# Statistics matmul of the norm behind the fourth instead of the second weight unit, in another PSUM bank

## The chip, the core and the metric

One core of a Trainium2 chip runs the whole kernel as one program. The metric is the device time in microseconds (us); three runs of the kernel before gave 2397.48, 2397.86 and 2401.97 us, median 2397.86 us.

## The reference, cut to what matters

512 tokens of width 1024 go through two blocks in a row. The first has an attention mixer, a SwiGLU feed-forward block, a second attention mixer and a second SwiGLU; the second has a gated linear recurrence and a retention layer. All is float32.

```
def rmsnorm(x, g):
    y = x * rsqrt(mean(x * x, -1) + RMS_EPS) * g
def swiglu(h, w_gu, w_down):
    gu = h @ w_gu;  g, u = gu[..., :D_FF], gu[..., D_FF:]      # D_FF = 2816
    return (silu(g) * u) @ w_down
# feed-forward, twice:      h = h + swiglu(rmsnorm(h, ffn_norm[i]), ...)
# retention, once:          h = rms_norm(x, norm_pre[1]);  u = h @ w_in   (q, k, v, gate of 4 heads)
```

Each norm needs, for every token, the sum of squares over the 1024 channels. The kernel multiplies by the gain before the matmul and by the token's reciprocal root after it, on the matmul's result. So the matmuls that use the normed x can begin before the sum of squares is known; only their evacuation from PSUM needs it.

## The kernel before, in words

**Layout.** The residual R is kept transposed: 8 tiles (k = 0 to 7) of 128 channels x 512 tokens. Each version of it is scaled by a gain and split in two float32r parts: XH (the high part, ScalarE, L1055) and XL (the rest, VectorE, L1560). A product takes three matmuls: high x high, low x high, high x low.

**Weights.** They come as "units" of 128 x 1024 float32 (512 KB). SyncE loads them in order into a ring of RING = 5 slots WR (L496); unit u may load once unit u-5 has been used (semaphore unit_used). ScalarE makes the high half WH (L1046), VectorE the low half WL (L1554). Both do so at places written out by hand: `split(end)` handles all units below `end` that have not been handled, and waits for each of them in order.

**TensorE.** `unit` (L505) runs one unit: 2 tiles k, 4 banks o, 3 matmuls each, so 24 matmuls of 128 x 128 x 512, all from L523. `group` runs several units that accumulate into the same 4 of the 8 PSUM banks. `x_ready` makes a group wait, tile by tile, for XH and XL. `between` is a table of calls made between units of a group. In both SwiGLU blocks (`swiglu(layer, ...)`) 11 groups of 4 units (units f+0 to f+43) are run, alternating between banks 0-3 and 4-7; layer 0 starts with banks 0-3, layer 1 with 4-7. The retention layer runs for each of 4 heads three groups of 4 units, the first into its `own` banks (0-3 for head 0), the second into the `other` banks.

**Sum of squares.** GpSimd squares the eight tiles of R one after the other and adds them up in SQS (`squares`, L1405 to L1411). `statistics` on TensorE waits until that is done (sq_sum) and multiplies SQS by a matrix of ones (L540), which puts the sum over the partitions into a PSUM bank; for the retention layer 8 narrow matmuls (L543) also put it, token by token on the partitions, into the bank behind it. VectorE reads both (`variance`, L1571), which raises rb_var; ScalarE takes the root (`root`, L1060), VectorE the reciprocal (`rstd`, L1575). Engines work strictly in program order, so `statistics` stops TensorE, if the squares are not there yet, and everything written behind it waits.

**Order around the change.** In group 0 of a SwiGLU `statistics` stands behind the second unit and writes into the first bank of the next group. Before group 1 TensorE waits for rb_var, since that group overwrites the bank. VectorE handles units up to f+5, reads the variance, takes the reciprocal, and only then units f+6 and f+7; ScalarE does likewise. In the retention layer it is the same with units R+0 to R+3, banks 6 and 7, and rb_var 8 awaited ahead of head 0's second group.

Of the kernel before, what the change touches and what calls it, by code (L numbers as in the profile page):

```python
# [13 lines left out]
T = 512  # L14
# [42 lines left out]
def program(nc, ws, x, vec, cst, sel, turn_a, turn_r, decay, post1, out):  # L57
    with ExitStack() as ctx:
# [13 lines left out]
        R = sb("R", [P, DT, T])  # L72
# [429 lines left out]

        @block.tensor
        def _(pe):
            def unit(u, kpair, hi, lo, bank, first, last, stationary, ready=None):  # L505

                s = u % RING
                pe.wait_ge(lo_ready, u + 1)
                for kk in range(2):
                    k = 2 * kpair + kk  # L510
                    if ready is not None:
                        ready(k)
                    for o in range(4):
                        if stationary:
                            cols = slice(kk * T + o * P, kk * T + (o + 1) * P)
                            pairs = [(WH[:, s, cols], hi[:, k, :]), (WH[:, s, cols], lo[:, k, :]),
                                     (WL[:, s, cols], hi[:, k, :])]
                        else:
                            cols = slice(kk * T, (kk + 1) * T)
                            xh, xl = stationary_x(hi, k, o), stationary_x(lo, k, o)  # L520
                            pairs = [(xh, WH[:, s, cols]), (xh, WL[:, s, cols]), (xl, WH[:, s, cols])]
                        for i, (l, r) in enumerate(pairs):
                            mm = pe.matmul(PS[:, bank + o, :], l, r, start=first and kk == 0 and i == 0,  # L523
                                           stop=last and kk == 1 and i == 2)
                mm.then_inc(unit_used, 1)
# [1 line left out]
            def stationary_x(t, k, o):  # L527
                return t[:, k, o * P:(o + 1) * P]

            def group(u, kpairs, hi, lo, bank, stationary=True, ready=None, between=None):  # L530

                for j in range(kpairs):
                    unit(u + j, j, hi, lo, bank, j == 0, j == kpairs - 1, stationary, ready)
                    if between is not None and j in between:
                        between[j]()

# [174 lines left out]
            for q in range(4):  # L711
# [6 lines left out]
                for kk in range(2):  # L718
# [12 lines left out]
                    for e in SPOT.get((6, 8 + 2 * q + kk), ()):  # L731
                        attend(e)

            def swiglu(layer, v, s):
                f, dn = U[f"F{layer}"], U[f"D{layer}"]
                first = 4 * layer
                for j in range(11):
                    n = 11 * layer + j
                    if j == 1:
                        pe.wait_ge(rb_var, s + 1)  # L740
                    if j >= 2:
                        pe.wait_ge(u_ready, n - 1)
                    group(f + 4 * j, 4, XH, XL, first if j % 2 == 0 else 4 - first, ready=x_ready(v),
                          between=None if j else {1: lambda: statistics(s, 4 - first)})
                pe.wait_ge(u_ready, 11 * layer + 10)

                def hidden(k):
                    pe.wait_ge(hh_ready, 11 * layer + k // 2 + 1)
                    pe.wait_ge(hl_ready, 11 * layer + k // 2 + 1)
                for d in range(2):  # L750
                    if d:
                        pe.wait_ge(u_ready, 11 * layer + 11)
                    group(dn + 11 * d, 11, HH, HL, first if d else 4 - first, ready=hidden)
# [232 lines left out]
            for h in range(RH):  # L986
                u = U["R"] + 12 * h
                own, other = own_banks(h), 4 - own_banks(h)

                group(u, 4, XH, XL, own, ready=x_ready(7),  # L990
                      between={1: lambda: outputs_turned(h - 1)} if h else {1: lambda: statistics(7, 6, (0,))})
                pe.wait_ge(rb_var, 8)
                if h:
                    pe.wait_ge(yl_ready, 4 * h)
                    pe.wait_ge(yh_ready, 4 * h)
                group(u + 4, 4, XH, XL, other, stationary=False)
                pe.wait_ge(rr_step, 4 * h + 4)
                group(u + 8, 4, XH, XL, own, stationary=False)
                pe.wait_ge(rr_ready, 4 * h + 4)
                pe.wait_ge(rsg_ready, 4 * h + 4)  # L1000
                pe.wait_ge(rg_ready, 4 * h + 4)
                for kb in range(TB):
                    for c in range(2):
                        mm = pe.matmul(PS[:, other + kb, 0:T - kb * P], R_QK[:, 2 + c, kb * P:(kb + 1) * P],
                                       R_QK[:, c, kb * P:T], start=c == 0, stop=c == 1)
                    mm.then_inc(rs_done, 1)
                pe.wait_ge(rv_ready, 4 * h + 4)
                for qb in range(TB):
                    pe.wait_ge(rpt_ready, 4 * h + qb + 1)
                    for kb in range(qb + 1):  # L1010
                        mm = pe.matmul(PS[:, own + qb, :],  # L1011
                                       R_PT[:, PT0[kb] + (qb - kb) * P:PT0[kb] + (qb - kb + 1) * P],
                                       R_V[:, kb, :], start=kb == 0, stop=kb == qb)
                    mm.then_inc(ro_done, 1)
# [23 lines left out]
        def _(act):  # L1038
            halved = [0]

            def split(end):

                for u in range(halved[0], min(end, UNITS)):
                    s = u % RING
                    act.wait_ge(landed[s], LANDED[u])
                    nc.scalar.activation(WH[:, s, :], WR[:, s, :], ACT.Copy).then_inc(hi_ready, 1)  # L1046
                halved[0] = max(halved[0], end)
# [100 lines left out]

            def swiglu(layer, s):
                f, dn = U[f"F{layer}"], U[f"D{layer}"]  # L1150
                split(f + 6)
                root(s)
                for j in range(11):
                    n = 11 * layer + j
                    split(f + 4 * j + 8)
                    act.wait_ge(g_ready, n + 1)
                    if j:
                        act.wait_ge(gs_ready, n)
                    nc.scalar.activation(F_S[:, :, :], F_G[:, :, :], ACT.Sigmoid).then_inc(sg_ready, 1)
                    act.wait_ge(ht_ready, n + 1)  # L1160
                    nc.scalar.activation(HH[:, 2 * j:2 * j + 2, :], F_U[:, :, :], ACT.Copy).then_inc(hh_ready, 1)
                split(dn + 15)
# [172 lines left out]
            for h in range(RH):  # L1335
# [4 lines left out]
                else:  # L1340
                    act.wait_ge(r_done, 56)
                act.dma_start(R_D[:, :], decay[h]).then_inc(decay_in, 16)
                split(u + 6)
                if h:
                    outputs_high(h - 1)
                else:
# [197 lines left out]
        def _(dve):  # L1544
# [22 lines left out]

            def variance(s, bank, width=T):
                dve.wait_ge(stat_done, s + 1)
                v = PS[:, bank:bank + 2, :].rearrange("p b t -> p (b t)")  # L1570
                ts(RB[:, 0:width], v[:, 0:width], 1.0 / D, RMS_EPS, ALU.mult, ALU.add).then_inc(rb_var, 1)  # L1571

            def rstd(s, width=T):
# [219 lines left out]
            def swiglu(layer, s):  # L1793
                f, dn = U[f"F{layer}"], U[f"D{layer}"]
                first = 4 * layer
                split(f + 6)
                variance(s, 4 - first)
                rstd(s)
                rb2 = RB[:, 0:T].unsqueeze(1).to_broadcast([P, 2, T])

                def low(j):
                    dve.wait_ge(hh_ready, 11 * layer + j + 1)
                    tt(HL[:, 2 * j:2 * j + 2, :], F_U[:, :, :], HH[:, 2 * j:2 * j + 2, :].bitcast(F32),
                       ALU.subtract).then_inc(hl_ready, 1)
                for j in range(11):
                    n = 11 * layer + j
                    bank = first if j % 2 == 0 else 4 - first
                    u = f + 4 * j
                    if j:
                        split(u + 6)  # L1810
                        low(j - 1)
                    split(u + 8)
                    dve.wait_ge(unit_used, u + 4)
                    tt(F_G[:, :, :], PS[:, bank:bank + 2, :], rb2, ALU.mult).then_inc(g_ready, 1)
                    if j:
                        dve.wait_ge(hl_ready, n)
                    tt(F_U[:, :, :], PS[:, bank + 2:bank + 4, :], rb2, ALU.mult).then_inc(u_ready, 1)
                    dve.wait_ge(sg_ready, n + 1)
                    tt(F_G[:, :, :], F_G[:, :, :], F_S[:, :, :], ALU.mult).then_inc(gs_ready, 1)  # L1819
                low(10)  # L1820
                return dn
# [248 lines left out]
            x_low(7, "pre1", 7)  # L2070


            split(U["R"] + 6)
            variance(7, 6, T + 4)
            rstd(7, T + 4)
            dve.wait_ge(rotr_in, 32)
# [195 lines left out]
```

## Time and profile before

| | |
|---|---|
| median of 3 runs | 2397.86 us |
| profiled execution, its own time | 2400.79 us |
| its span in the trace | 2399.0 us |
| mean granted TensorE clock | 0.971 of 2.4 GHz |
| PE busy (matmul) | 2247.3 us, 94% |
| DVE (VectorE) busy | 1222.0 us, 51% |
| ACT (ScalarE) busy | 798.3 us, 33% |
| POOL (GpSimd) busy | 532.7 us, 22% |
| DMA | 198.27 MB, mean 83 GB/s |

PE's busy time is of pipelined matmuls with modelled ends: a float32r matmul of 512 columns reads 0.39 us, but the next starts 0.227 us after it. So distances between starts say more than durations. Behind the span lie 1.8 us (2400.79 - 2399.0) of the execution that the trace does not cover.

### The profile page before, as it was taken

What the parts mean: (1) busy time and instruction counts of PE and PEld (TensorE: products, weight loads), DVE (VectorE), ACT (ScalarE), POOL (GpSimd) and SP (SyncE); (2) the same over time, 40 slices, a digit from 0 to 9 for tenths busy, and PEclk for the clock granted to TensorE, in tenths of its full rate; (3) what the DMA queues carried; (4) which work ended last, traced back from release to release, by engine and by line L of the source; (5) the groups of instructions that cost most, each with busy time, mean ns of one, the idle gap of its engine ahead of it and who ended that gap; (6) DMA issues with size and microseconds to landing.
All of it is one profiled execution on the core that took longest, in us unless ns stands there. A gap on an engine that the chain in (4) does not pass through costs nothing.

```text
span 2399.0 us, 26711 instructions
## 1 busy us (share of the span) xinstructions
PE 2247.3 (94%) x10598; PEld 1801.3 (75%) x10598; DVE 1222.0 (51%) x1987; ACT 798.3 (33%) x1334; POOL 532.7 (22%) x355
## 2 busy tenths in 40 slices
PE   7999999998899999999998999998994969999997
PEld 6788876886688888876666888887773748777876
DVE  5655556565544433554455444326858664444342
ACT  3334323442322222233432222213446423333321
POOL 2533334231410101222233011034125030000000
PEclk9999999998999999999999999999997989999999
DMA  4222221221233333332222333332331212222322
GB/s 139 88 62 80 80 80 54 71 80 45 71 97 97 97 97 98 96 97 89 71 61 72 97 97 97 98 97 79 94 91 44 79 57 88 75 75 78 93 74 76
DMA packets 84155, 198.27 MB, mean 83 GB/s; under 512 B 7216, under 2 KB 44208, under 8 KB 84032
## 3 DMA queue, kind: packets, MB, share of 16 engines
q1 hardware_dynamic: 81408, 189.62, 26.0%
q10 hardware_dynamic: 2624, 6.93, 0.9%
q8 instruction: 86, 1.41, 0.2%
q14 instruction: 37, 0.30, 0.0%
HBM read 194.40 MB, written 2.13 MB: 82 GB/s over the span
## 4 chain that ended last, share of the span: by engine, by line
PE 81%; DVE 9%; issue 4%; ACT 3%; POOL 3%; DMA 0%; DVEq 0%; SPq 0%; POOLq 0%; ACTq 0%
PE PS L523 49%; PE PS L567 5%; PE PS L569 5%; PE PS L568 5%; PE PS L592 2%; PE PS L593 2%; PE PS L594 2%; PE PS L1011 1%; PE PS L640 1%; PE PS L650 1%; PE PS L664 1%; DVE WL L1554 1%; POOL SQS L1411 1%; POOL SQT L1409 1%; PE PS L879 1%
## 5 line engine op out<-in xcount | busy, mean ns | idle before, releaser
L1554 DVE TENSOR_TENSOR WL<-WR,WH 128x1024 fp32r<-128x1024 f32 x353 | 475.2, 1354 | 786.3 <-ACT WH L1046 785.6
L1046 ACT ACTIVATE WH<-WR 128x1024 fp32r<-128x1024 f32 x353 | 370.0, 1056 | 732.2 <-DMA WR<-in_ws 723.1
L523 PE MATMUL PS<-XH,WH 128*128 128x512 f32 x1024 | 406.7, 397 | 18.9 <-ACT XH L1055 10.5
L523 PE MATMUL PS<-XL,WH 128*128 128x512 f32 x1024 | 402.3, 393 | 0.0
L523 PE MATMUL PS<-XH,WL 128*128 128x512 f32 x1024 | 402.0, 393 | 0.0
L523 PEld LDWEIGHTS PS<-XH,WH 128*128 128x128 f32 x1024 | 195.0, 190 | 65.1 <-issue 20.4
L567 PE MATMUL PS<-XH,WH 128*128 128x512 f32 x544 | 224.1, 412 | 5.0 <-DVE WL L1554 3.6
L523 PEld LDWEIGHTS PS<-XL,WH 128*128 128x128 f32 x1024 | 194.9, 190 | 41.6 <-issue 1.7
L523 PEld LDWEIGHTS PS<-XH,WL 128*128 128x128 f32 x1024 | 194.5, 190 | 41.2
L569 PE MATMUL PS<-XH,WL 128*128 128x512 f32 x544 | 214.6, 395 | 0.0
L568 PE MATMUL PS<-XL,WH 128*128 128x512 f32 x544 | 214.1, 393 | 0.0
L1466 POOL TENSOR_TENSOR F_U<-F_G,F_U 128x1024 f32<-128x1024 f32 x22 | 52.7, 2393 | 424.0 <-DVE F_G L1819 424.0
L1444 POOL TENSOR_TENSOR A_SH<-A_SH,A_SIN 128x512 f32<-128x512 f32 x48 | 82.2, 1713 | 268.9 <-DVE A_SH L1739 268.9
L523 PE MATMUL PS<-HH,WH 128*128 128x512 f32 x352 | 136.9, 389 | 0.0
L523 PE MATMUL PS<-HL,WH 128*128 128x512 f32 x352 | 136.9, 389 | 0.0
L523 PE MATMUL PS<-HH,WL 128*128 128x512 f32 x352 | 136.9, 389 | 0.0
L567 PEld LDWEIGHTS PS<-XH,WH 128*128 128x128 f32 x544 | 104.0, 191 | 27.4 <-issue 4.6
L1076 ACT ACTIVATE A_P<-A_P,A_ST 128x128 f32<-128x128 f32 (+1 forms) x192 | 79.7, 416 | 132.0 <-DVE A_ST L1682 132.0
L569 PEld LDWEIGHTS PS<-XH,WL 128*128 128x128 f32 x544 | 103.3, 190 | 23.2
L568 PEld LDWEIGHTS PS<-XL,WH 128*128 128x128 f32 x544 | 103.8, 191 | 18.9
L523 PE MATMUL PS<-WH,XH 128*128 128x512 f32 x256 | 99.6, 389 | 0.0
L523 PE MATMUL PS<-WL,XH 128*128 128x512 f32 x256 | 99.6, 389 | 0.0
(332 smaller groups left out, 3771.5 us busy)
## 6 DMA issues: line engine op xcount, KB each, us to landing
WR<-in_ws SPq DMA_DIRECT2D x281, 512.0 KB, 3.6
WR<-in_ws SPq DMA_DIRECT2D x144, 256.0 KB, 3.2
B_CB<-gates ACTq DMA_DIRECT2D x8, 512.0 KB, 3.9
XTOK<-in_x SPq DMA_DIRECT2D x2, 1024.0 KB, 8.3
out<-OUT SPq DMA_DIRECT2D x4, 512.0 KB, 2.6
R_D<-in_decay ACTq DMA_DIRECT2D x4, 256.0 KB, 2.6
GAIN<-in_post ACTq DMA_DIRECT2D x1, 512.0 KB, 5.4
CST<-in_cst SPq DMA_DIRECT2D x1, 320.0 KB, 3.4
```

The lines of the kernel that those rows point to most:

```text
L523: mm = pe.matmul(PS[:, bank + o, :], l, r, start=first and kk == 0 and i == 0, stop=last and kk == 1 and i == 2)
L567: pe.matmul(PS[:, bank + o, :], WH[:, s, cols], hi[:, k, :], start=first, stop=False)
L568: pe.matmul(PS[:, bank + o, :], WH[:, s, cols], lo[:, k, :], start=False, stop=False)
L569: return pe.matmul(PS[:, bank + o, :], WL[:, s, cols], hi[:, k, :], start=False, stop=last)
L592: pe.matmul(PS[:, o, :], xh, wh, start=first and kk == 0, stop=False)
L593: pe.matmul(PS[:, o, :], xh, wl, start=False, stop=False)
L594: mm = pe.matmul(PS[:, o, :], xl, wh, start=False, stop=last and kk == 1)
L1046: nc.scalar.activation(WH[:, s, :], WR[:, s, :], ACT.Copy).then_inc(hi_ready, 1)
L1076: x = nc.scalar.activation(A_P[:, n % 2, h, w], A_P[:, n % 2, h, w], ACT.Exp, bias=stat(m, 0, 2 * pair + h, qb), accum_out=stat(m, 1, 2 * ...
L1444: nc.gpsimd.tensor_tensor(A_SH[:, r % 2, :], A_SH[:, r % 2, :], A_SIN[:, :], ALU.mult).then_inc(rot_m, 1)
L1466: nc.gpsimd.tensor_tensor(F_U[:, :, :], F_G[:, :, :], F_U[:, :, :], ALU.mult).then_inc(ht_ready, 1)
L1554: tt(WL[:, s, :], WR[:, s, :], WH[:, s, :].bitcast(F32), ALU.subtract).then_inc(lo_ready, 1)
```

## The change

In both SwiGLU blocks and in the retention layer `statistics` is called behind the fourth unit of the first group instead of behind the second (`between` index 3 instead of 1). In the SwiGLU blocks it writes into the last bank of the next group (7 in layer 0, 3 in layer 1) instead of the first (4 and 0). The wait for rb_var is no longer ahead of the next group: `unit` calls `free(o)` before the first matmul into each bank, and the wait is made only at the bank that holds the sums (o = 3 in the SwiGLU blocks; o = 2, which is bank 6, in the retention layer). ScalarE and VectorE handle the weight units up to f+7 (R+7) instead of f+5 (R+5) before root and variance. `variance` reads one bank instead of naming two where only 512 columns are used.

```diff
-            def unit(u, kpair, hi, lo, bank, first, last, stationary, ready=None):
+            def unit(u, kpair, hi, lo, bank, first, last, stationary, ready=None, free=None):
...
                     for o in range(4):
+                        if free is not None and first and kk == 0:
+                            free(o)
...
+            def variance_read(o, count):
+
+                def wait(bank):
+                    if bank == o:
+                        pe.wait_ge(rb_var, count)
+                return wait
+
             def swiglu(layer, v, s):
...
-                    if j == 1:
-                        pe.wait_ge(rb_var, s + 1)
                     if j >= 2:
                         pe.wait_ge(u_ready, n - 1)
                     group(f + 4 * j, 4, XH, XL, first if j % 2 == 0 else 4 - first, ready=x_ready(v),
-                          between=None if j else {1: lambda: statistics(s, 4 - first)})
+                          between=None if j else {3: lambda: statistics(s, 7 - first)},
+                          free=variance_read(3, s + 1) if j == 1 else None)
...
                 group(u, 4, XH, XL, own, ready=x_ready(7),
-                      between={1: lambda: outputs_turned(h - 1)} if h else {1: lambda: statistics(7, 6, (0,))})
-                pe.wait_ge(rb_var, 8)
+                      between={1: lambda: outputs_turned(h - 1)} if h else {3: lambda: statistics(7, 6, (0,))})
...
-                group(u + 4, 4, XH, XL, other, stationary=False)
+                group(u + 4, 4, XH, XL, other, stationary=False, free=None if h else variance_read(2, 8))
...
             def swiglu(layer, s):                       # ScalarE
-                split(f + 6)
+                split(f + 8)
                 root(s)
...
-                split(u + 6)
+                split(u + 6 if h else u + 8)
...
             def variance(s, bank, width=T):
-                v = PS[:, bank:bank + 2, :].rearrange("p b t -> p (b t)")
+                v = PS[:, bank:bank + 1 + (width > T), :].rearrange("p b t -> p (b t)")
...
             def swiglu(layer, s):                       # VectorE
-                split(f + 6)
-                variance(s, 4 - first)
+                split(f + 8)
+                variance(s, 7 - first)
...
-            split(U["R"] + 6)
+            split(U["R"] + 8)
             variance(7, 6, T + 4)
```

## Rows read from the trace of the kernel before

**Rows 1.** The page: shares of the chain that ended last, by engine
```profile
PE 81%; DVE 9%; issue 4%; ACT 3%; POOL 3%; DMA 0%; DVEq 0%; SPq 0%; POOLq 0%; ACTq 0%
```
**Rows 2.** Waits of PE: who for whom, us in total, times, longest us
```profile
PE PS L540 <- POOL SQS L1411: 28.6, 3, 10.9
```
**Rows 3.** Timeline, PE, layer 0: start us, duration us, operation [idle before, releaser]
```profile
625.73 0.39 PE L523 MATMUL PS<-XH,WL 128*128 128x512 f32 x1
634.81 2.07 PE L540 MATMUL PS<-SQS,CST 128*128 128x512 f32 x2 [8.69 <-POOL SQS L1411]
...
637.86 0.39 PE L523 MATMUL PS<-XH,WH 128*128 128x512 f32 x1
...
642.39 0.39 PE L523 MATMUL PS<-XH,WL 128*128 128x512 f32 x1
```
**Rows 4.** Timeline, PE and DVE, layer 1: the same place
```profile
1267.28 0.39 PE L523 MATMUL PS<-XH,WL 128*128 128x512 f32 x1
1276.75 2.07 PE L540 MATMUL PS<-SQS,CST 128*128 128x512 f32 x2 [9.08 <-POOL SQS L1411]
...
1283.34 0.39 PE L523 MATMUL PS<-XH,WH 128*128 128x512 f32 x1
...
1270.20 4.26 DVE L1554 TENSOR_TENSOR WL<-WR,WH 128x1024 fp32r<-128x1024 f32 x2
```
**Rows 5.** Timeline, PE, retention layer: tile k = 3, the statistics, the second group
```profile
1960.40 0.47 PE L523 MATMUL PS<-XH,WH 128*128 128x512 f32 x1 [0.81 <-ACT XH L1055]
...
1974.24 2.08 PE L540 MATMUL PS<-SQS,CST 128*128 128x512 f32 x2 [10.87 <-POOL SQS L1411]
...
1990.95 0.39 PE L523 MATMUL PS<-WH,XH 128*128 128x512 f32 x1
```
**Rows 6.** The chain in order of time, the piece behind layer 0's statistics: start, us
```profile
636.88 348.62 PE PS L523 x1536
```
**Rows 7.** Timeline, PE: the second attention's statistics, which meet no wait
```profile
1001.66 1.02 PE L540 MATMUL PS<-SQS,CST 128*128 128x512 f32 x2
1002.52 0.95 PE L543 MATMUL PS<-CST,SQS 128*128 128x1 f32 x8
...
1003.64 0.39 PE L568 MATMUL PS<-XL,WH 128*128 128x512 f32 x1
```
**Rows 8.** Timeline, DVE and ACT, layer 0: lowered units, variance, unit f+7
```profile
626.86 4.26 DVE L1554 TENSOR_TENSOR WL<-WR,WH 128x1024 fp32r<-128x1024 f32 x2
636.92 0.69 DVE L1571 TENSOR_SCALAR RB<-PS 128x512 f32<-128x512 f32 x1 [5.80 <-PE PS L540]
...
646.19 1.06 ACT L1046 ACTIVATE WH<-WR 128x1024 fp32r<-128x1024 f32 x1 [6.97 <-DMA WR<-in_ws]
```
**Rows 9.** Tile SQS: the adds on POOL, ns shortest/median/longest, first and last start us
```profile
L1411 POOL TENSOR_TENSOR SQS<-SQS,SQT x28: 1260/1620/2163, 613.7 to 1972.6; 128x512 f32<-128x512 f32 x28
```
**Rows 10.** Timeline, DVE, retention layer: XL of k = 3, 5, 6, 7, then two units
```profile
1959.51 0.74 DVE L1560 SCALAR_TENSOR_TENSOR XL<-R,VC,XH 128x512 fp32r<-128x512 f32 x1
...
1967.10 0.74 DVE L1560 SCALAR_TENSOR_TENSOR XL<-R,VC,XH 128x512 fp32r<-128x512 f32 x1
...
1970.87 0.74 DVE L1560 SCALAR_TENSOR_TENSOR XL<-R,VC,XH 128x512 fp32r<-128x512 f32 x1
1971.74 1.32 DVE L1560 SCALAR_TENSOR_TENSOR XL<-R,VC,XH 128x512 fp32r<-128x512 f32 x1
1973.43 2.97 DVE L1554 TENSOR_TENSOR WL<-WR,WH 128x1024 fp32r<-128x1024 f32 x2 [0.37 <-ACT WH L1046]
```
**Rows 11.** DMA issues from 1960 to 1985 us: count, KB each, median us to landing
```profile
WR<-in_ws SPq DMA_DIRECT2D x1, 512.0 KB, 3.5
...
R_D<-in_decay ACTq DMA_DIRECT2D x1, 256.0 KB, 3.7
```
**Rows 12.** Windows, retention layer: length, busy PE, PEld, DVE, ACT, POOL; clock, DMA, GB/s
```profile
1956.00:1963.00 7.00, 5.66 (x25) 4.35 (x24) 6.93 (x6) 1.26 (x2) 6.06 (x4) 1.00 0.26 77
1977.50:1982.50 5.00, 5.00 (x13) 3.95 (x14) 3.96 (x2) 1.58 (x2) 0.00 (x0) 0.50 0.00 0
```

More of the change, by code:

```diff
@@ L528, in stationary_x, with group @@
                 return t[:, k, o * P:(o + 1) * P]
-            def group(u, kpairs, hi, lo, bank, stationary=True, ready=None, between=None):
+            def group(u, kpairs, hi, lo, bank, stationary=True, ready=None, between=None, free=None):
                 for j in range(kpairs):
-                    unit(u + j, j, hi, lo, bank, j == 0, j == kpairs - 1, stationary, ready)
+                    unit(u + j, j, hi, lo, bank, j == 0, j == kpairs - 1, stationary, ready, free)
                     if between is not None and j in between:
```

## Prediction, made before the changed kernel was run

> **What bounds the kernel now.** I first read the chain of work that ended last: 81% of the span is TensorE (PE) work [rows 1], so a microsecond counts where PE stands still, or runs at its low clock. Next came the waits of PE. The longest is that of `statistics` (L540) for the sum of squares that GpSimd (POOL) adds up (L1411): 28.6 us in three places [rows 2]. The timelines give each place. In layer 0 the last matmul of the second unit starts at 625.73 and the next thing PE does is L540 at 634.81, the moment POOL is done [rows 3]; in layer 1 it is 1267.28 and 1276.75 [rows 4]; in the retention layer PE waits from the end of tile k = 3 until 1974.24 [rows 5]. What stands behind L540 in PE's order are the third and fourth unit of the group, which need nothing of the sum. So the reader is to see three holes with ready work queued behind them. Each hole also has a tail: PE restarts at its low clock. From 1977.50 to 1982.50 the granted clock is 0.50, that is 1.2 GHz, and 13 matmuls take 5.00 us [rows 12].
>
> **The pace of PE.** At the high clock (2.4 GHz) 20 starts take 642.39 - 637.86 = 4.53 us [rows 3], so a slot is 0.2265 us, a tile (12 matmuls) 2.72 us and a unit (24) 5.44 us.
>
> **Layer 0.** Without the wait the third unit starts at 625.73 + 0.23 = 625.96, and its fourth matmul at 625.96 + 3 x 0.2265 = 626.64. Before, that matmul starts at 637.86 [rows 3]: 11.22 us lost, which is 8.85 of standing and 2.37 of cold statistics and restart. Now the statistics run behind the fourth unit on a warm PE. There L540 takes 1002.52 - 1001.66 = 0.86 us up to the next start [rows 7]. Gain 11.22 - 0.86 = 10.36 us.
>
> Are the inputs there? The XL tiles are all done by 626.86, when VectorE (DVE) starts the two units behind them [rows 8]; the last tile, k = 7, is needed at 625.96 + 3 x 2.72 = 634.12. The units f+2 and f+3 were lowered before f+4 and f+5. The fourth unit ends at 625.96 + 2 x 5.44 = 636.84; POOL is done at 634.81. Margin 2.0 us, so `statistics` no longer waits.
>
> **Layer 1.** The thirteenth matmul behind the hole starts at 1283.34; without it, it would start at 1267.51 + 12 x 0.2265 = 1270.23 [rows 4]. Lost: 13.11 us. Gain 13.11 - 0.86 = 12.25 us. Tile 7 is ready at 1270.20 [rows 4] and needed at 1275.7; the fourth unit ends at 1278.39, POOL at 1276.75: margin 1.6 us.
>
> **Retention layer.** Here X itself comes slowly: DVE makes an XL tile every 3.8 us, more than the 2.72 us that PE needs for it. PE starts a tile 0.15 us behind XL's end (1959.51 + 0.74 = 1960.25, PE at 1960.40) [rows 5, 10]. So tile 5 starts at 1967.84 + 0.15 = 1967.99 and ends at 1970.71; tile 6 starts at 1971.61 + 0.15 = 1971.76 and ends at 1974.48; tile 7 (XL done at 1973.06) follows at once and ends at 1977.20. POOL has been done since 1974.24: here the hole goes because X ends last, 3 us later than POOL. Statistics with the 8 narrow matmuls cost, warm, 1003.64 - 1001.66 - 0.23 = 1.75 us [rows 7]. The second group starts at 1978.95, before at 1990.95 [rows 5]. Gain 12.0 us.
>
> **The wait that is moved.** rb_var is now awaited inside the next group, ahead of the bank with the sums, and DVE has to get there first. Behind that wait PE has the whole rest of the group. DVE's order is now: units f+6 and f+7, then the variance. f+7 may load only when unit f+2 has been used (ring of 5). In layer 0 that unit ends at 631.57 (start of its last matmul + 0.39). Before, the same step took 646.19 - (642.39 + 0.39) = 3.41 us from release to ScalarE's (ACT) start [rows 3, 8], and a weight load lands in 3.5 us [rows 11]. So ACT starts f+7 at 634.98, and is done at 636.04; DVE lowers it in 1.2 to 2.1 us (a contended one is 4.26 / 2 = 2.13 [rows 8]; POOL is finished, so I take 1.2) to 637.3. PE ends the statistics at 637.86 at the latest, the variance takes 0.69 us [rows 8]: rb_var at 638.6. PE is at bank 3 (9 matmuls on) at 637.70 + 2.04 = 639.74. Margin 1.1 us, the same in layer 1: cost nothing. The load, cast and lowering of f+6 come forward too, off the path. In the retention layer unit R+2 ends at 1970.9, and ACT issues three 256 KB tables just then. Alone, R+7 lands in 3.5 us (1974.4); behind one of them it would take 3.5 + 3.7 = 7.2 us (1978.1) [rows 11]. DVE has R+4 and R+5 done at 1976.40 [rows 10], R+6 and R+7 at 1978.8 if landed early, 1980.5 if late. rb_var is then up at 1979.7 or at 1981.2, and PE is at bank 6 (6 matmuls on) at 1978.95 + 1.36 = 1980.31. Cost 0 to 0.9 us; I take 0: R+7 was released 0.1 us ahead of the tables, so it is nearer to the 3.5 us of a load alone.
>
> The waits at the banks themselves are checked at three places between matmuls; x_ready puts two ahead of every tile of a first group, and the 0.2265 us pace has them in it. I take nothing for them, at most 0.1 us. Less reading of PSUM in `variance` changes nothing, since its output stays 512 wide.
>
> **Beside POOL.** What comes forward on DVE is the lowering of f+6 at 631.1, beside POOL's last instructions. An add on POOL takes 1.26 us alone and 2.16 at its longest [rows 9]; if the last two instructions both grow by 0.9, POOL ends at 636.6 in layer 0, still ahead of 636.84. In layer 1 only the last add can grow: 1277.7 against 1278.39. Cost nothing.
>
> The Trainium skill speaks against that: SBUF — State Buffer, section "Who interferes with whom", says that DVE with two SBUF inputs and GpSimd take a shared port pair as an exclusive lock, the second fully blocked. By that rule two of POOL's instructions would each wait out one lowering of 1.2 us, POOL would end 0.4 us behind PE in layer 0, and the gain would be smaller by that. The row of adds, 1.26 to 2.16, agrees with waiting of that size, so the rule moves the end by tenths only.
>
> **What follows behind.** PE's work behind layer 0's statistics is one unbroken piece of 348.62 us [rows 6]; all that feeds it is released by PE itself, so it moves forward whole. Next to be late would be u_ready, group 0's evacuation, which the third group awaits. Before, DVE began it behind unit f+7, at 646.19 + 1.06 + 1.2 = 648.5 [rows 8]. Even if it stayed there, that is 11 us ahead of the third group's new start at 637.70 + 4 x 5.44 = 659.5.
>
> **The sum.** 10.36 + 12.25 + 12.0 = 34.6 us. The profiled execution took 2400.79 us and would take 2366.2. The median of the runs is 2.9 us below it; the three gains are taken off it alike: 2397.86 - 34.6 = 2363.3 us.
>
> **The rivals.**
>
> A: PE loses its clock in the retention layer. With tiles fed every 3.8 us PE pauses about 1.1 us ahead of each. Before, it did so at k = 2 and 3 too, and the clock from 1956 to 1963 was 1.00 with PE busy 5.66 of 7 us [rows 12]; that speaks against it. For it: the pauses now go on over tiles 4 to 6. Price: at 13 matmuls in 5.00 us (a wave of 0.43 us at half clock) a tile takes 5.1 us, more than the 3.8 of X, so tiles 4 to 7 end at 1964.2 + 4 x 5.1 = 1984.6 instead of 1977.2, 7.4 us later: 2370.7 us.
> The Trainium skill has such a rule: TensorE: Matmul & The Clock Gate, section "A second HAM failure mode: psum-queue depth-cycling", tells that frequent micro-idles between groups of matmuls make the clock swing. The row at 1.00 does not bear it out here.
>
> B: the weights come late for the variance, so that the old wait is replaced by one inside the next group. Price 0.9 us in the retention layer, by the bounds above, and perhaps 1 more in each feed-forward block: up to 2366 us.
>
> C: the time is given back: PE arrives early somewhere where another engine sets the pace. For it: ACT and DVE do the same work in less time. Against: they are busy 33% and 51%, and the unbroken piece [rows 6]. Price: all, 2397.9 us.
>
> D, slower than before: the variance on DVE now stands behind unit f+7, whose load is released only by the third unit of the same group. If it lands late, PE stands at bank 3 just as long. From 3.5 + 1.1 = 4.6 us on each us costs one; at 4.6 + 11.5 = 16.1 us the gain is gone in each of the three places; at 20 us it would be 3.9 us slower in each, 2409.6 us. Against it: loads land in 3.5 us, the slowest of these rows in 3.7 [rows 11].
>
> E: the change does not do what it says, if POOL ended later than the fourth unit. The margins are 2.0, 1.6 and 3.0 us.
>
> **Chances.** Forecast 0.79, A 0.07, B 0.09 (a shift of 1 to 3 us), C 0.03, D 0.02; E only shrinks the gain and lies in the forecast's range. Range: the cold tails vary with the phase of the clock, 2.37 us in layer 0 against 13.11 - 9.24 = 3.87 in layer 1. Were all tails like the long one, the gain would be 1.5 us larger; like the short one, some 3 smaller. The runs of before differ by 4.5 us. So 2360.0 to 2369.0 us. What a measurement of this kernel can tell from no change is about 0.2%, 4.8 us; faster by more 0.95, within 0.03, slower 0.02.
>
> **What would show it.** Right: no wait of L540 for L1411 longer than 0.5 us; the matmuls of third and fourth unit at 0.227 us from the second; L540 at 1.02 us instead of 2.07; the retention layer's statistics at 1977.2 less the 22.6 us gained earlier, that is 1954.6; clock 1.00 in the three stretches. Wrong: PE waiting for RB at bank 3 or 6 (B, D); a clock of 0.50 ahead of the retention statistics (A); new waits of L523 for WL or for u_ready (C).

## The result

The changed kernel takes 2364.72 us (median of 4 runs, 2361.93 to 2366.95), the kernel before 2398.64 us (4 runs, 2397.48 to 2401.97): ratio 0.9856, 95% interval 0.9839 to 0.9873. It is 33.9 us faster; the prediction said 34.6 (2363.3 us, range 2360.0 to 2369.0). The profiled execution took 2365.22 us, its span is 2363.4 us. The line numbers are those of the changed kernel: L540 is now L542, L523 L525, L1411 L1418, L1554 L1561, L1571 L1578.

The page of the changed kernel: busy time by engine, then the chain by engine. PE is as busy in us as before, within 9 us of 2247.3; POOL has gone from 3% of the chain [rows 1] to 0%, "issue" from 4% to 2%.

```profile
PE 2238.7 (95%) x10598; PEld 1797.5 (76%) x10598; DVE 1225.6 (52%) x1987; ACT 798.2 (34%) x1334; POOL 536.0 (23%) x355
...
PE 85%; DVE 9%; ACT 3%; issue 2%; DMA 0%; POOL 0%; DVEq 0%; SPq 0%; ACTq 0%
```

The waits of PE, longest first (who for whom, total us, times, longest). The wait of `statistics` for POOL, 28.6 us before [rows 2], is in no line any more, and none for RB at L1578 has taken its place. What is first now stood second before, in the recurrence; the wait for XH (three waits, 10.5 us) has grown to five of 12.0 us together, by the pauses between tiles in the retention layer.

```profile
PE PS L961 <- ACT L_R L1295: 14.8, 1, 14.8
PE PS L525 <- ACT L_IB L1295: 14.8, 1, 14.8
PE PS L525 <- ACT XH L1062: 12.0, 5, 9.2
```

The timeline of PE and DVE in layer 0, to be held against [rows 3, 8]. The statistics (L542) follow the fourth unit without a gap and take 1.02 us, not 2.07; the second group's second matmul is at 639.70, one slot of 0.23 us behind where its first belongs (638.61 + 0.86 = 639.47). DVE reads the variance from 639.66 to 640.35, while PE is at bank 3 only at 641.55.

```profile
638.37 0.40 PE L525 MATMUL PS<-XH,WL 128*128 128x512 f32 x1
638.61 1.02 PE L542 MATMUL PS<-SQS,CST 128*128 128x512 f32 x2
639.06 0.80 PE L525 MATMUL PS<-XH,WH 128*128 128x512 f32 x1
639.70 0.40 PE L525 MATMUL PS<-XL,WH 128*128 128x512 f32 x1
...
641.55 0.39 PE L525 MATMUL PS<-XH,WH 128*128 128x512 f32 x1
...
637.65 1.23 DVE L1561 TENSOR_TENSOR WL<-WR,WH 128x1024 fp32r<-128x1024 f32 x1 [2.71 <-ACT WH L1053]
639.66 0.69 DVE L1578 TENSOR_SCALAR RB<-PS 128x512 f32<-128x512 f32 x1 [0.79 <-PE PS L542]
```

The same in the retention layer, to be held against [rows 5, 10]: the second group starts one slot ahead of 1955.59 (1955.36); PE reaches bank 6 at 1956.75, 0.6 us after DVE's variance (1955.45 + 0.70 = 1956.15). The variance itself waited 0.46 us for PE's statistics, not for a weight unit.

```profile
1953.61 1.02 PE L542 MATMUL PS<-SQS,CST 128*128 128x512 f32 x2
1954.47 0.95 PE L545 MATMUL PS<-CST,SQS 128*128 128x1 f32 x8
1955.28 0.48 PE L525 MATMUL PS<-WH,XH 128*128 128x512 f32 x1
1955.59 0.39 PE L525 MATMUL PS<-WL,XH 128*128 128x512 f32 x1
...
1956.75 0.39 PE L525 MATMUL PS<-WH,XH 128*128 128x512 f32 x1
...
1955.45 0.70 DVE L1578 TENSOR_SCALAR RB<-PS 128x516 f32<-128x516 f32 x1 [0.46 <-PE PS L545]
```

The windows of the three places in the changed kernel (length, busy PE, PEld, DVE, ACT, POOL, granted clock, DMA share, GB/s): clock 1.00 in each.

```profile
616.00:639.00 23.00, 23.00 (x102) 18.90 (x101) 19.97 (x16) 9.77 (x11) 19.88 (x13) 1.00 0.28 92
1247.00:1269.00 22.00, 22.00 (x98) 18.03 (x97) 20.48 (x15) 9.46 (x11) 19.41 (x12) 1.00 0.31 96
1936.00:1954.00 18.00, 15.19 (x63) 11.34 (x62) 17.37 (x15) 6.76 (x8) 12.32 (x8) 1.00 0.33 112
```

Where the 35.6 us between the two spans (2399.0 - 2363.4) come from, by the starts of the groups in both timelines:

| from first matmul of group 1 to that of group 2 | before | after | gain | predicted |
|---|---|---|---|---|
| layer 0 | 615.08 to 648.05: 32.97 | 616.84 to 639.47: 22.63 | 10.3 | 10.36 |
| layer 1 | 1256.63 to 1291.50: 34.87 | 1246.59 to 1269.22: 22.63 | 12.2 | 12.25 |
| retention | 1948.99 to 1990.95: 41.96 | 1925.22 to 1955.36: 30.14 | 11.8 | 12.0 |

(Starts behind the shown rows are carried on by 0.2265 us a slot.) The three places gave 34.4 us. The other 1.2 us lie between them, where nothing was changed: 1.8 us more ahead of layer 0, 1.5 less between layers 0 and 1, 1.5 less between layer 1 and the retention layer, 0.0 behind it. What moved there was not looked into.

### The profile page after: what moved, and what is told of

It reads as the page before. It is cut to its first block, busy times and chain, and to the rows that moved or that the text cites. A ratio compares the mean times of both kernels' runs of the same rounds, so it can differ in the third digit from the quotient of the medians.

```text
span 2363.4 us, 26705 instructions
## 1 busy us (share of the span) xinstructions
PE 2238.7 (95%) x10598; PEld 1797.5 (76%) x10598; DVE 1225.6 (52%) x1987; ACT 798.2 (34%) x1334; POOL 536.0 (23%) x355
## 4 chain that ended last, share of the span: by engine, by line
PE 85%; DVE 9%; ACT 3%; issue 2%; DMA 0%; POOL 0%; DVEq 0%; SPq 0%; ACTq 0%
PE PS L525 50%; PE PS L569 5%; PE PS L571 5%; PE PS L570 5%; PE PS L594 2%; PE PS L595 2%; PE PS L596 2%; PE PS L1018 1%; PE PS L642 1%; PE PS L652 1%; PE PS L666 1%; DVE WL L1561 1%; PE PS L897 1%; PE PS L887 1%; ACT WH L1053 1%
## 5 line engine op out<-in xcount | busy, mean ns | idle before, releaser
L1561 DVE TENSOR_TENSOR WL<-WR,WH 128x1024 fp32r<-128x1024 f32 x353 | 478.3, 1365 | 759.0 <-ACT WH L1053 758.3
L525 PE MATMUL PS<-XH,WH 128*128 128x512 f32 x1024 | 404.8, 395 | 20.4 <-ACT XH L1062 12.0
L525 PE MATMUL PS<-XH,WL 128*128 128x512 f32 x1024 | 401.5, 392 | 0.0
L525 PE MATMUL PS<-XL,WH 128*128 128x512 f32 x1024 | 401.3, 392 | 0.0
L525 PEld LDWEIGHTS PS<-XH,WH 128*128 128x128 f32 x1024 | 194.1, 190 | 66.1 <-issue 21.1
L525 PEld LDWEIGHTS PS<-XL,WH 128*128 128x128 f32 x1024 | 194.1, 190 | 41.1 <-issue 1.2
L525 PEld LDWEIGHTS PS<-XH,WL 128*128 128x128 f32 x1024 | 193.9, 189 | 40.9
L525 PE MATMUL PS<-HH,WL 128*128 128x512 f32 x352 | 137.0, 389 | 0.0
L525 PE MATMUL PS<-HL,WH 128*128 128x512 f32 x352 | 137.0, 389 | 0.0
L525 PE MATMUL PS<-HH,WH 128*128 128x512 f32 x352 | 137.0, 389 | 0.0
L525 PE MATMUL PS<-WH,XH 128*128 128x512 f32 x256 | 99.7, 390 | 0.0
L525 PE MATMUL PS<-WL,XH 128*128 128x512 f32 x256 | 99.7, 389 | 0.0
```

The costliest lines, as they stand in the source:

```text
L1561: tt(WL[:, s, :], WR[:, s, :], WH[:, s, :].bitcast(F32), ALU.subtract).then_inc(lo_ready, 1)
```

## The experiments

Each is timed against the kernel before on the same chip; its median there was 2398.72 us for the first four, 2397.9 us for the next four, 2399.39 us for the last three. Edits are against the changed kernel unless said otherwise.

**1. The feed-forward blocks alone** (retention layer as before).

```diff
-      ... else {3: lambda: statistics(7, 6, (0,))})
+      ... else {1: lambda: statistics(7, 6, (0,))})
+                pe.wait_ge(rb_var, 8)
-                group(u + 4, ..., free=None if h else variance_read(2, 8))
+                group(u + 4, ...)
-                split(u + 6 if h else u + 8)      # and VectorE: split(U["R"] + 8)
+                split(u + 6)                      # and split(U["R"] + 6)
```

> The change in the two feed-forward blocks only; the retention layer is as before. Theory (each place gives its own hole and tail, and nothing downstream gives it back): 10.4 + 12.3 = 22.6 us less than before, 2376 us; PE waits for the sum of squares once, about 11 us, in the retention layer. Rival C (time is given back further on): clearly less than 22 us here, or more than the whole change minus this in the other half.

Measured: 2376.84 us, ratio 0.9911 [0.9897, 0.9926], 21.9 us less. One wait for the sum is left:

```profile
PE PS L542 <- POOL SQS L1419: 10.9, 1, 10.9
```

**2. The retention layer alone.** In the feed-forward blocks `statistics` stands behind the second unit again; its sums still go into the last bank, and the wait for them stays at that bank.

```diff
-                          between=None if j else {3: lambda: statistics(s, 7 - first)},
+                          between=None if j else {1: lambda: statistics(s, 7 - first)},
-                split(f + 8)                      # ScalarE and VectorE
+                split(f + 6)
```

> The change in the retention layer only. Theory: 12.0 us less than before, 2386.6 us, and two waits of PE for the sum of squares of 8.7 and 9.1 us stay. With the run that changes the feed-forward blocks alone the gains add up to that of the whole change, 34 us. Rival C: the two gains do not add up.

Measured: 2387.31 us, ratio 0.9952 [0.9937, 0.9967], 11.4 us less. 21.9 + 11.4 = 33.3 us against 33.9 for the whole: the gains add up, as nearly as intervals of 3 to 4 us on either side of each can tell. Rival C, that time is given back, falls: the table above has nothing given back behind the last place either.

**3. Behind the third unit.**

```diff
-   {3: lambda: statistics(...)}    split(f + 8), split(U["R"] + 8)
+   {2: lambda: statistics(...)}    split(f + 7), split(U["R"] + 7)
```

> Statistics behind the third unit instead of the fourth at all three places, ScalarE and VectorE taking one unit less ahead of the variance. Theory (what counts is whether PE has work until GpSimd is done): GpSimd is 3.4 to 4.2 us late in each feed-forward block, 3.5 in the retention layer where 2.5 of it remain, so 10 to 11 us of the gain go: 2375 us; up to 2382 us if the clock falls to 0.5 in these short holes as in the long ones. Rival (any later place does): 2365 us as with the whole change.

Measured: 2382.08 us, ratio 0.9927 [0.9913, 0.9942]: half of the gain is gone, at the upper end of what was expected. The waits are short, 11.8 us in all, but behind each of them PE runs at its low clock for a while all the same (waits, a timeline row, and the window behind the hole in layer 0, clock 0.50):

```profile
PE PS L542 <- POOL SQS L1418: 11.8, 3, 4.5
...
635.23 2.08 PE L542 MATMUL PS<-SQS,CST 128*128 128x512 f32 x2 [3.99 <-POOL SQS L1418]
...
635.50:639.50 4.00, 4.00 (x8) 2.48 (x9) 1.46 (x2) 1.43 (x2) 0.00 (x0) 0.50 0.00 0
```

Here the tenth matmul behind L542 starts at about 640.9, on a warm PE it would be 635.23 + 0.86 + 9 x 0.2265 = 638.13: a tail of 2.8 us behind a hole of 4, where holes of 9 us had tails of 1.5 and 3.0.

**4. Sums in the first bank.** The whole change, but in the feed-forward blocks PE waits at bank 0.

```diff
-   {3: lambda: statistics(s, 7 - first)}    variance_read(3, s + 1)    variance(s, 7 - first)
+   {3: lambda: statistics(s, 4 - first)}    variance_read(0, s + 1)    variance(s, 4 - first)
```

> The whole change, but in the feed-forward blocks the sums go into the first bank of the next group, so that PE waits for the variance ahead of that group's first matmul. Theory: statistics end 0.2 us behind the next slot of PE, the variance takes 0.7 us and a semaphore 0.1: PE stands 0.9 to 1.0 us in each of two places, clock stays at 1.00, 2366.6 us. Rival (the last bank is what makes the gain, since the wait would otherwise take the place of the old one): 3 us or more per place, 2371 us or above.

Measured: 2366.23 us, ratio 0.9862 [0.9846, 0.9879], by time not to be told from the change. The trace shows the price: two waits for RB, 1.8 us together, one of them here.

```profile
PE PS L525 <- DVE RB L1578: 1.8, 2, 0.9
...
639.78 0.47 PE L525 MATMUL PS<-XH,WH 128*128 128x512 f32 x1 [0.88 <-DVE RB L1578]
```

The first matmul behind such a pause reads 0.47 us, not 0.77 as behind the 9.21 us wait at 1925.22 in the changed kernel, and the next follow at 0.23 us: the clock has stayed high. The bank is worth 1.8 us of 34, the place of the call the rest.

**5. The holes filled, nothing moved.** The kernel before, with PE kept busy.

```diff
+            def warm(bank, count):
+                for _ in range(count):
+                    pe.matmul(PS[:, bank, :], XH[:, 0, 0:P], XH[:, 0, :], start=True, stop=True)
-   {1: lambda: statistics(s, 4 - first)}
+   {1: lambda: (pe.wait_ge(x_hi, 8 * v + 5), warm(4 - first, 36), statistics(s, 4 - first))}
-   {1: lambda: statistics(7, 6, (0,))}
+   {1: lambda: (warm(6, 46), statistics(7, 6, (0,)))}
```

> The kernel before, with nothing moved, but TensorE fills each of the three holes ahead of the statistics with matmuls nobody reads (36, 36 and 46 of 512 columns, about 8.2, 8.2 and 10.4 us). The waits stay as long. Theory (part of the gain is the restart at the low clock): 1.5 + 3.0 + 4.1 = 8.6 us less than before, 2390 us, L540 at 1.02 us, clock 1.00 behind it. Rival (the holes alone count): 2398.7 us.

Measured: 2391.84 us, ratio 0.9971 [0.9961, 0.9981], that is 4.6 to 9.4 us less; the expected 8.6 lies in it. The window of the hole in layer 0, of the kernel before and then of this one:

```profile
626.00:640.00 14.00, 5.31 (x16) 3.58 (x16) 7.50 (x5) 3.90 (x5) 8.23 (x6) 0.76 0.13 37
```
```profile
626.00:640.00 14.00, 13.51 (x58) 10.54 (x57) 8.39 (x5) 3.51 (x4) 7.93 (x6) 1.00 0.10 38
```

Same useful work, same wait for POOL, another clock. The trace gives the tails place by place: from the first matmul of group 1 to that of group 2 it is 1.4, 2.8 and 3.9 us less than in the kernel before (in the retention layer 1980.69 - 1942.63 = 38.06 against 41.96), 8.1 in all. So of the 34 us some 5 to 9 are the restart at the low clock; the rest is standing. Waits and tails, 28.6 + 8.1 us, are more than the 34.4 gained, since in the retention layer PE now spends some of the time in the pauses between tiles of X.

**6. One unit more ahead of the variance.**

```diff
-   split(f + 8)    split(u + 6 if h else u + 8)    split(U["R"] + 8)
+   split(f + 9)    split(u + 6 if h else u + 9)    split(U["R"] + 9)
```

> The whole change, but ScalarE and VectorE take one unit more (f+8, R+8) ahead of root and variance. That unit loads only when the fourth unit of the first group is used. Theory (rival D's mechanism of the prediction is real, its price is the lateness of rb_var): rb_var comes 3.7 us behind TensorE's arrival at the bank in all three places, 11 us lost, 2376 us; up to 7 us more if the clock falls. Rival (that order does not matter): 2365 us.

Measured: 2384.02 us, ratio 0.9938 [0.9917, 0.9958]; the profiled execution took 2379.65 us. Three waits of 3.7, 3.5 and 3.5 us, as long as computed. Behind those of the feed-forward blocks the clock falls (0.50 in the window from 642.4); behind the third, in the retention layer, it was 1.00 (window from 1970).

```profile
PE PS L525 <- DVE RB L1578: 10.7, 3, 3.7
...
642.41 0.80 PE L525 MATMUL PS<-XH,WH 128*128 128x512 f32 x1 [3.74 <-DVE RB L1578]
...
642.40:647.50 5.10, 5.09 (x12) 4.07 (x13) 4.41 (x2) 1.91 (x2) 0.00 (x0) 0.50 0.02 5
...
1970.00:1975.00 5.00, 4.06 (x18) 3.35 (x19) 4.27 (x3) 0.63 (x1) 0.00 (x0) 1.00 0.01 3
```

Rival D's mechanism is real: a unit whose load is released too late inside the group must not stand ahead of the variance. With unit f+8 ahead of it only 13.9 us of gain remain instead of 33.9; with f+7 as the last, as in the change, there are 0.6 to 1.2 us to spare. The median is 1 us above the expected 2376 to 2383.

**7. Units lowered behind the reciprocal, as before.**

```diff
-   split(f + 8)    split(u + 6 if h else u + 8)    split(U["R"] + 8)
+   split(f + 6)    split(u + 6)                    split(U["R"] + 6)
```

> The whole change without moving units f+6, f+7 (R+6, R+7) ahead of root and variance: they come behind the reciprocal as before. Theory: that part of the change is worth nothing, 2365 us; GpSimd ends its sum about 0.8 us earlier against TensorE in each feed-forward block, since no lowering runs beside its last instructions, and TensorE waits nowhere for RB. Rival (the units have to be ahead, else TensorE waits for the low half of f+6): 2368 us or more with a wait of L525 for L1561.

Measured: 2365.75 us, ratio 0.9859 [0.9843, 0.9875]: not to be told from the change. No wait for a low half came of it. This part of the change is worth nothing that these runs can show. It does slow POOL: the last square in layer 0 takes 1.84 us in the changed kernel (first row) and 1.04 in this one (second).

```profile
634.00 1.84 POOL L1416 TENSOR_TENSOR SQT<-R 128x512 f32<-128x512 f32 x1
```
```profile
631.73 1.04 POOL L1416 TENSOR_TENSOR SQT<-R 128x512 f32<-128x512 f32 x1
```

**8. ScalarE squares in the retention layer.**

```diff
             def build_x(v, version, gain, before, ks=range(DT)):
...
+                    if v == 7:
+                        nc.scalar.activation(L_G[:, k, :], R[:, k, :], ACT.Square).then_inc(sq_mul, 1)
...
-            squares(7, R, residual(6), 6)
+            pool.wait_ge(stat_done, 7)
+            for k in range(1, DT):
+                pool.wait_ge(sq_mul, 48 + k + 1)
+                pool.wait_ge(sq_sum, 41 + k)
+                so_far = L_G[:, 0, :] if k == 1 else SQS[:, :]
+                nc.gpsimd.tensor_tensor(SQS[:, :], so_far, L_G[:, k, :], ALU.add).then_inc(sq_sum, 1)
```

> The whole change, and in the retention layer ScalarE squares the eight tiles; GpSimd only adds them (1 instruction per tile instead of 2). Theory (with the hole gone, what sets the end of the first group is the X tile every 3.8 us, and that pace is VectorE slowed beside GpSimd): VectorE's tile comes at 2.7 us or less, TensorE sets the pace, the first group is 4.2 us shorter: 2360.5 us. Rival (VectorE's own work sets 3.8 us): 2365 us.

Measured: 2360.39 us, ratio 0.9837 [0.9822, 0.9853]. Why X came slowly: VectorE's scaling of a tile (the instruction that writes L_O) in the changed kernel beside POOL, then two in this one, the first with POOL idle, the second beside its add.

```profile
1928.79 1.52 DVE L2072 SCALAR_TENSOR_TENSOR L_O<-L_O,VC,RB 128x512 f32<-128x512 f32 x1
```
```profile
1931.67 0.75 DVE L2079 SCALAR_TENSOR_TENSOR L_O<-L_O,VC,RB 128x512 f32<-128x512 f32 x1
...
1934.76 1.77 DVE L2079 SCALAR_TENSOR_TENSOR L_O<-L_O,VC,RB 128x512 f32<-128x512 f32 x1
```

The mechanism holds, the size of a step does not: tiles come every 3.1 us on average, not 2.7 or less, since the add still meets every other tile. So X still sets the pace here, not TensorE; that the time is the expected 2360.5 us all the same is partly luck.

**9. The same with R+6, R+7 behind the reciprocal.** Edit 8 and the retention part of edit 7.

> The whole change with ScalarE's squares in the retention layer, and units R+6, R+7 lowered behind the reciprocal again. In the run with the squares alone TensorE stood 0.2 us at bank 6, because R+7 landed late for the variance. Theory: that goes and nothing else moves, 2360.2 us, not to be told from 2360.4 by time, but no wait of L525 for RB. Rival (the lowering is missed behind): a new wait of L525 for the low half, 2361 us or more.

Measured: 2360.11 us, ratio 0.9836 [0.9822, 0.9849], and no wait of L525 for RB at L1585.

**10. The same with a warm start.** Edit 9, and 38 matmuls in the 9 us ahead of the first tile.

```diff
+            pe.wait_ge(lo_copied, 2)
+            pe.wait_ge(lo_ready, U["R"] + 1)
+            for _ in range(38):
+                pe.matmul(PS[:, 1, :], WH[:, U["R"] % RING, 0:P], WH[:, U["R"] % RING, 0:T], start=True, stop=True)
```

> As squares_later, and TensorE fills the 9 us ahead of the retention layer's first tile with 38 matmuls nobody reads, so that it starts at the high clock. Theory (with a tile of X every 3.1 us and 2.7 us of matmuls for it, a warm start only makes TensorE wait for X): group 1 ends 0.1 to 0.2 us earlier, 2360 us; the waits for XH and XL grow by some 2 us. Rival (the cold start counts, as it did in the filled holes): 2.4 us less, 2357.8 us.

Measured: 2361.81 us, ratio 0.9844 [0.9831, 0.9857], not faster. The start was warm: windows from the first tile on, of run 9 (clock 0.84) and of run 10 (1.00).

```profile
1924.00:1934.00 10.00, 9.77 (x37) 8.05 (x38) 9.90 (x11) 4.43 (x8) 6.13 (x4) 0.84 0.17 50
```
```profile
1925.00:1950.00 25.00, 24.43 (x102) 18.22 (x101) 22.43 (x23) 10.88 (x17) 11.30 (x7) 1.00 0.30 95
```

From VectorE's variance of the norm before to the retention layer's statistics it is 1948.31 - 1915.78 = 32.53 us in run 9 and 1950.15 - 1917.59 = 32.56 in run 10 (run 9 first):

```profile
1915.78 0.69 DVE L1585 TENSOR_SCALAR RB<-PS 128x512 f32<-128x512 f32 x1 [1.34 <-PE PS L976]
...
1948.31 1.02 PE L542 MATMUL PS<-SQS,CST 128*128 128x512 f32 x2
```
```profile
1917.59 0.69 DVE L1590 TENSOR_SCALAR RB<-PS 128x512 f32<-128x512 f32 x1 [1.34 <-PE PS L976]
...
1950.15 1.02 PE L542 MATMUL PS<-SQS,CST 128*128 128x512 f32 x2
```

So the low clock costs nothing at this place, where X sets the pace; at the three holes of the kernel before, where PE had its input, it did (experiment 5).

**11. The changed kernel again**, beside 9 and 10.

> The changed kernel again, beside the two others on the same chip: 2364.7 us, 4.3 us above them if the gain of the squares on ScalarE is real, the same if that was the spread of the runs.

Measured: 2366.0 us, ratio 0.9861 [0.9847, 0.9874]. Run 9 is 5.9 us below it; of these the first group's length explains 4.3 (30.14 us in the changed kernel, 25.8 in run 9, where it starts at 1924.23 and the second at 1948.31 + 1.75 = 1950.06). The two profiled executions lie 4.1 us apart in their spans (2362.3 and 2358.2); the other 1.6 us of the medians are not explained. Run 9 beats both kernels.

## Why the prediction was right, point by point

**The holes and their tails.** Right in each place to 0.2 us (table above). The step that carried it was to count, from the timeline, to the first matmul at full pace behind the hole and not to the end of the wait: the waits alone are 28.6 us, and filling them without shortening them (experiment 5) brings the tails on top.

**Margins of POOL.** Direction right, size a little off. The prediction had 2.0 and 1.6 us and let POOL grow by up to 1.8 and 0.9 beside VectorE. In layer 0 one instruction grew, not two: the last square by 0.8 us (experiment 7), the add behind it took 1.29. POOL ended at 635.92 + 1.29 = 637.21, PE came at 638.61, margin 1.4. In layer 1 the last add grew by 0.9; POOL ended at 1265.44 + 2.15 = 1267.59, PE came at 1268.35, margin 0.8.

```profile
635.92 1.29 POOL L1418 TENSOR_TENSOR SQS<-SQS,SQT 128x512 f32<-128x512 f32 x1
...
1265.44 2.15 POOL L1418 TENSOR_TENSOR SQS<-SQS,SQT 128x512 f32<-128x512 f32 x1
...
1268.35 1.02 PE L542 MATMUL PS<-SQS,CST 128*128 128x512 f32 x2
```

By the rule of an exclusive port (the Trainium skill, SBUF — State Buffer, "Who interferes with whom") the prediction had two instructions in layer 0 wait 1.2 us each and POOL end 0.4 us behind PE. Only one was slowed, so POOL ended ahead of PE without speaking against the rule: 0.8 to 0.9 us more an instruction, beside a lowering that takes 1.23 us alone, agrees with waiting for much of one.

**The moved wait.** Right: margins 1.2 us in layer 0 and 0.6 in the retention layer, predicted 1.1 and 0.6. The load of R+7 was 4.6 us from its release to ScalarE's start at 1951.81, between the bounds of 1950.7 and 1954.4 (the end of unit R+2 at 1947.24 and the predicted 3.5 and 7.2 us), nearer to the short one, as chosen, though 1.1 us behind it. The tables beside it landed later too: R_COS took 4.5 us where it had taken 2.6.

**Rival A** (low clock in the retention layer): fell, clock 1.00 from 1936 to 1954 with PE busy 15.19 of 18 us. Pauses of 0.8 us between tiles did not lower the clock. One of its figures was read loosely: 13 matmuls in 5.00 us [rows 12] would be 0.385 us each, not 0.43. The window touches 13, but in the timeline of that stretch starts are 0.427 us apart (nine steps from 1978.24 to 1982.08), and the tile of 5.1 us goes by that. **Rivals B and E**: none of the waits they name is there. **Rival C** fell with experiments 1 and 2, **rival D** is real as a mechanism (experiment 6) and was not met.

**The end of group 1 in the retention layer.** "The hole goes because X ends last" held: experiment 8 sped up X and the end moved.

**The signs.** The retention layer's statistics came at 1953.61, predicted 1954.6. The 1.0 us is what the stretches between the places gave (1.2), less 0.2 by which the first group was longer.

**The range.** 2360.0 to 2369.0 us held all runs of the changed kernel. The median is 1.4 us above the forecast: 0.7 us less was gained (33.9 against 34.6), and the kernel before, run once more, had a median 0.8 us higher than the one that the sum started from. Both are smaller than the spread of its runs, so a hit as close as this is in part luck; the 0.2 us in each place, read from starts in the traces, is not.

## What to carry to other kernels

Price a wait on TensorE up to the first matmul at full pace, not to its end: even 4 us waits were followed by a stretch at half clock (experiments 3 and 6), though one of 3.5 us was not. A reduction whose result only the evacuation needs belongs behind enough ready work to cover it; here that took the fourth unit, the third was not enough. Its result in a bank that is overwritten later saves a little more, 1.8 us of 34 here. Before casts or loads are put ahead of the reader of that result in the same queue, ask which of them is released only inside the running group: one unit further cost 20 us of 34.

## What the runs showed that was not expected

GpSimd's adds slow VectorE even where they are the only GpSimd work left: 0.75 us for a scaling of 128 x 512 with POOL idle, 1.77 beside an add. Taking the squares away from GpSimd therefore shortened the tile from 3.8 to only 3.1 us. And the runs of experiment 6 spread over 9.7 us (2379.65 to 2389.31), against 5.0 for the changed kernel. Their mean granted clocks go with their times: 0.977, 0.976, 0.975 and 0.973 from the shortest to the longest. So how long PE stays at its low clock behind the same waits seems to differ from run to run; only the shortest of the four has a trace, and it is not shown at which of the waits. Short holes alone do not make the spread: experiment 3, with three of them, had 3.6 us.
